# A streaming-encoder trunk: state products in four quadrants of TensorE, a shorter lift of the scan, Toeplitz rows copied in three parts

## The reference

```python
lam_bar = jnp.exp(lam * step)                       # 64 groups x 64 complex states
b_bar = ((lam_bar - 1.0) / lam)[..., None] * b
bu = jnp.einsum('blgn,gpn->blgp', uf, b_bar)        # 16 inputs of a group into its 64 states
_, states = lax.associative_scan(combine, (a, bu), axis=1)      # s[t] = lam_bar * s[t-1] + bu[t]
y = jnp.einsum('gnp,blgp->blgn', c, states).real + d * uf
y = jax.nn.gelu(y.reshape(bsz, seq, D_MODEL))
y = y * jax.nn.sigmoid(y @ glu_w + glu_b)           # the first large product, "GLU"
```

## Time and profile before

| | before |
|---|---|
| median of 3 runs | 1282.84 us |
| the profiled execution, whole | 1282.2 us |
| its span, first to last instruction | 1280.4 us |
| TensorE busy in the span | 97% |
| VectorE, ScalarE, GpSimd busy | 52%, 36%, 5% |
| mean granted TensorE clock | 0.997 of full |
| start of the first GLU product in the span | 105.53 us |

### The profile page before, as it was taken

One profiled execution on the slowest core, in us unless ns is written; L12 is line 12 of the kernel. 1 busy time (PEld: TensorE's weight loads), 2 busy tenths in 40 slices (PEclk: granted clock), 3 DMA queues, 4 the chain that ended last, 5 costly groups with the idle time before them and its releaser, 6 DMA issues.

```text
span 1280.4 us, 16011 instructions
## 1 busy us (share of the span) xinstructions
PE 1247.4 (97%) x6277; PEld 1041.6 (81%) x6277; DVE 671.6 (52%) x785; ACT 462.1 (36%) x486; POOL 64.5 (5%) x79
## 2 busy tenths in 40 slices
PE   3899999999999999999999999999999999999998
PEld 3788888888888888888888888888888888888886
DVE  8996854444444444646556465644454444444443
ACT  5635533333333333333333333422333333332232
POOL 6940000000000000000000000000000000000000
PEclk9999999999999999999999999999999999999999
DMA  5374233232323334322222232223232333323331
GB/s 115 100 133 133 67 117 106 77 104 87 100 76 91 93 109 138 107 66 96 77 81 91 66 106 81 84 84 92 87 106 91 99 98 98 98 68 90 92 110 67
DMA packets 148207, 121.03 MB, mean 95 GB/s; under 512 B 5720, under 2 KB 141072, under 8 KB 148176
## 3 DMA queue, kind: packets, MB, share of 16 engines
q1 hardware_dynamic: 142416, 116.40, 29.6%
q10 hardware_dynamic: 5760, 4.20, 1.7%
HBM read 114.29 MB, written 2.10 MB: 91 GB/s over the span
## 4 chain that ended last, share of the span: by engine, by line
PE 94%; DVE 4%; ACT 1%; issue 0%; DMA 0%; SPq 0%; DVEq 0%
PE bank L701 27%; PE bank L703 27%; PE bank L702 27%; PE bank L800 2%; PE bank L801 2%; PE bank L799 2%; PE bank L647 1%; DVE bank L1169 1%; PE bank L829 1%; PE bank L827 1%; PE bank L828 1%; PE bank L838 1%; ACT s_states L892 1%; PE bank L812 0%; PE bank L813 0%; PE bank L528 0%
## 5 line engine op out<-in xcount | busy, mean ns | idle before, releaser
L701 PE MATMUL bank<-u_hi,w_hi 128*128 128x512 f32 x960 | 375.0, 391 | 0.0
L703 PE MATMUL bank<-u_hi,w_lo 128*128 128x512 f32 x960 | 373.5, 389 | 0.0
L702 PE MATMUL bank<-u_lo,w_hi 128*128 128x512 f32 x960 | 373.5, 389 | 0.0
L1179 DVE TENSOR_TENSOR w_lo<-w_raw,w_hi 128x2048 fp32r<-128x2048 f32 x112 | 256.5, 2290 | 170.3 <-ACT w_hi L892 170.2
L892 ACT ACTIVATE w_hi<-w_raw 128x2048 fp32r<-128x2048 f32 x112 | 213.9, 1910 | 322.3 <-PE bank L703 314.0
L701 PEld LDWEIGHTS bank<-u_hi,w_hi 128*128 128x128 f32 x960 | 180.3, 188 | 37.7 <-issue 0.9
L703 PEld LDWEIGHTS bank<-u_hi,w_lo 128*128 128x128 f32 x960 | 180.2, 188 | 37.7
L702 PEld LDWEIGHTS bank<-u_lo,w_hi 128*128 128x128 f32 x960 | 180.3, 188 | 37.5 <-issue 0.5
L701 PE MATMUL bank<-h_hi,w_hi 128*128 128x512 f32 x352 | 136.9, 389 | 0.0
L702 PE MATMUL bank<-h_lo,w_hi 128*128 128x512 f32 x352 | 136.9, 389 | 0.0
L703 PE MATMUL bank<-h_hi,w_lo 128*128 128x512 f32 x352 | 136.9, 389 | 0.0
(11 more groups left out here) (223 smaller groups left out, 1335.9 us busy)
## 6 DMA issues: line engine op xcount, KB each, us to landing
w_raw<-in_ret_w_qkvg_dram SPq DMA_DIRECT2D x24, 1024.0 KB, 5.0
w_raw<-in_ffn_w_gate_dram SPq DMA_DIRECT2D x22, 1024.0 KB, 5.2
w_raw<-in_ffn_w_up_dram SPq DMA_DIRECT2D x22, 1024.0 KB, 5.2
w_raw<-in_ffn_w_down_dram SPq DMA_DIRECT2D x32, 704.0 KB, 4.3
w_raw<-in_ret_w_o_dram SPq DMA_DIRECT2D x8, 1024.0 KB, 5.1
w_raw<-in_s_glu_w_dram SPq DMA_DIRECT2D x4, 1024.0 KB, 5.6
s<-in_x_dram ACTq DMA_DIRECT2D x8, 256.0 KB, 8.1
s_w<-in_x_dram SPq DMA_DIRECT2D x1, 2048.0 KB, 7.7
```

The lines of the kernel that those rows point to most:

```text
L701: pe.matmul(o, w_hi[w][:, w_cols], hi, start=first, stop=False)
L702: pe.matmul(o, w_hi[w][:, w_cols], lo, start=False, stop=False)
L703: return pe.matmul(o, w_lo[w][:, w_cols], hi, start=False, stop=end)
L1179: dve.tensor_tensor(w_lo[s][:, :], w_raw[:, s, :], w_hi[s][:, :].bitcast(F32), ALU.subtract).then_inc(w_lo_ready[s], 1)
```

## The change

- **State products.** `y_states(quarter, k)` now takes blocks k and k + 2 together. Of blocks 2, 3, 6 and 7 (`swapped`) the output halves are exchanged, so that four matmuls in a row go to four different 64 x 64 quadrants of the array, the two blocks writing two banks. `y_bank` undoes the exchange when the transposed block is read. `SLOT` orders the pairs in `states` so that a quarter of the lift holds blocks 0 and 2, 1 and 3, 4 and 6, 5 and 7.
- **Carries.** They are kept in a small array of their own, `carries`, and GpSimd copies them back to the ends of the segments (2 copies, `ends_ready`, for which `y_states` waits too).
- **Lift.** Three products in place of four: (re + im of the carry) times the real factor, and the carry times the sum and the difference of the factors (`lift_pair`, made before the scan). As instructions: one of 392 elements, three of 784.
- **Segment powers** come one block earlier on GpSimd, ahead of block 2's table, and are copied in the slots' order by 4 small copies. VectorE waits for them before the scan, and makes both `step8` and `step64` there.
- **Toeplitz rows** in three parts, of blocks 0 to 3, 4 and 5, 6 and 7. Both halves of part 0 are SP's, 16 DMAs of 128 KB; of parts 1 and 2 ScalarE issues half 1, 8 DMAs of 64 KB each. The strip of part 0 lies on partitions 0 to 31 over both slots of `w_raw`, those of parts 1 and 2 in slot 1.
- **Weights.** GLU weights go to slot 0 as soon as part 0 has landed, ahead of part 2's DMAs; to slot 1 after parts 1 and 2. VectorE's share of the split of slot 0 comes after `y_low(3)`, ScalarE's after `y_high(3)`.
- **Order.** TensorE: `strips(6)` first, then `y_inputs` 0 to 3, `strips(7)`, `y_inputs` 4, 5, then the two first quarters, `y_transposed` 0 to 3, `y_inputs` 6, 7, the two last quarters, `y_transposed` 4 to 7. The GELUs go 0, 2, 1, 3, 4, 6, 5, 7.

```diff
+SLOT = [0, 2, 1, 3, 4, 6, 5, 7]
-PART = 2 * JB
-NPART = J // PART
+PART_BLOCKS = [(0, 1, 2, 3), (4, 5), (6, 7)]
+PART_OF = [0, 0, 0, 0, 1, 1, 2, 2]
...
-            for part in range(NPART):
-                toeplitz_half(sp, part, 0)
-            for s in range(2):
-                for part in (s, 2 + s):
-                    sp.wait_ge(toep_loaded[part], 16 * 2 * STEPS)
-                load_unit(s, 0, glu_v[:, :, 256 * s:256 * s + 256], KT, 256)
+            toeplitz_half(sp, 0, 0)
+            toeplitz_half(sp, 0, 1)
+            toeplitz_half(sp, 1, 0)
+            sp.wait_ge(toep_loaded[0], 16 * 2 * STEPS)
+            load_unit(0, 0, glu_v[:, :, 0:256], KT, 256)
+            toeplitz_half(sp, 2, 0)
+            for part in (1, 2):
+                sp.wait_ge(toep_loaded[part], 16 * 2 * STEPS)
+            load_unit(1, 0, glu_v[:, :, 256:512], KT, 256)
...
-                        yield 4 * k + i, half, rows64, bank[S5_AT[("y", k)][0]][rows64, P * i:P * i + P]
+                        out0 = 64 * (half ^ swapped(k))
+                        yield 4 * k + i, half, rows64, bank[S5_AT[("y", k)][0]][out0:out0 + 64, P * i:P * i + P]
...
+            def y_states(quarter, k):
+                pe.wait_ge(ends_ready, 2)
+                pe.wait_ge(scan_done, quarter + 1)
+                both = [list(y_pairs(n)) for n in (k, k + 2)]
                 for i in range(4):
                     for ri in range(2):
-                        for jj, half, rows64, o in list(y_pairs(k))[2 * i:2 * i + 2]:
-                            mm = pe.matmul(o, states[rows64, 0:CH, ri, jj], r_tc[rows64, ri, jj, :, :],
+                        for n in range(2):
+                            for jj, half, rows64, o in both[n][2 * i:2 * i + 2]:
+                                at = JB * SLOT[jj // JB] + jj % JB
+                                mm = pe.matmul(o, states[rows64, 0:CH, ri, at], r_tc[rows64, ri, jj, :, :],
...
+            dve.wait_ge(lift_ready, 1)
+            rotation(step8, seg_powers[:, :, 0, :])
+            step(dve.tensor_copy(step64[:, 0], repeated(last_lift[:, 0], 2, 2)))
+            step(dve.tensor_copy(step64[:, 1, :, 0], last_lift[:, 1]))
+            step(dve.tensor_scalar(step64[:, 1, :, 1], last_lift[:, 1], -1.0, None, ALU.mult))
...
+            step(dve.tensor_tensor(lift_pair[:, :, 0, :], lift[1], lift[0], ALU.subtract))
+            step(dve.scalar_tensor_tensor(out=lift_pair[:, :, 1, :], in0=lift[0], scalar=-1.0, in1=lift[1],
...
-            dve.wait_ge(lift_ready, 1)
-            rotation(step64, seg_powers[:, :, SEG - 1, :])
...
+            step(dve.tensor_copy(carries[:, :, 0], ends[:, 0]))
...
+            step(dve.tensor_tensor(carry_sum, carries[:, :, :, 0, :], carries[:, :, :, 1, :], ALU.add))
...
+                step(mul(lift_re, repeated(carry_sum[:, part], 2, M), repeated(seg_powers[:, 0, 0:M, js], 1, M)))
+                step(mul(lift_im, repeated(carries[:, part], 2, M), repeated(lift_pair[:, :, :, js], 1, M)))
+                settle()
+                into = seg[:, 1:SEG, 0:M, :, js]
+                step(dve.tensor_tensor(into, into, repeated(lift_re, 3, 2), ALU.add))
+                settle()
+                dve.tensor_tensor(into, into, lift_im[:, :, :, ::-1, :], ALU.add).then_inc(scan_done, 1)
...
-                if n == 3:
+                if n == 2:
                     segment_powers()
```

More of the change, by code:

```diff
@@ L409, in tile, with swapped, y_bank @@
             return t[:, bass.ds(k, 1), :].rearrange("p o a -> p (o a)")
+        def swapped(k):
+            return k // 2 % 2
         def y_part(t, k):
             jb = k // 2
[L415 removed]
+            whole = t[:, jb:jb + 5:4, :].rearrange("p h (c t) -> p h c t", t=STEPS)
+            return whole[:, :, :, 4 * (k % 2):4 * (k % 2) + 4]
+        def y_bank(k):
+            ps = bank[S5_AT[("yt", k)][0]].rearrange("p (t h c) -> p h c t", t=4, h=2)
+            return ps[:, ::-1, :, :] if swapped(k) else ps
         def toeplitz_half(queue, part, half):
[L419 removed]
+            for k in PART_BLOCKS[part]:
                 b, fill = S5_AT[("strip", k)]
                 queue.wait_ge(bank_free[b], fill + 1)
[L422 to L423 removed]
+            g0 = J * half + JB * PART_BLOCKS[part][0]
+            n = JB * len(PART_BLOCKS[part])
             for r in range(STEPS):
                 at = LEAD - N * r
[L426 to L427 removed]
+                queue.dma_start(toep[N * r:N * r + N, g0:g0 + n, :],
+                                strip[part][N * half:N * half + N, :, at:at + P]).then_inc(toep_loaded[part], 16)
         @block.sync
@@ L666, in y_inputs @@
                     pe.matmul(o, u[:, jj, half, :], toep[:, J * half + jj, :], start=(jj % 4 == 0), stop=False)
+            strips(6)
             pe.wait_ge(toep_loaded[0], 16 * 2 * STEPS)
@@ L670, in _ @@
             y_inputs(1)
-            strips(6)
             pe.wait_ge(seg_done, 1)
-            pe.wait_ge(toep_loaded[1], 16 * 2 * STEPS)
             y_inputs(2)
@@ L1014, in y_high @@
                 ps, _ = s5_full("yt", k)
-                copy(y_part(g_hi, k), ps[:, :].rearrange("p (t h c) -> p h c t", t=4, h=2)).then_inc(y_hi_ready, 1)
+                copy(y_part(g_hi, k), y_bank(k)).then_inc(y_hi_ready, 1)
+            for k in (0, 2, 1, 3):
+                gelu(k)
             for k in range(4):
-                gelu(k)
+                y_high(k)
             split_weights(0, 0)
-            for k in range(4, 8):
-                if k % 2 == 0:
-                    y_high(k - 4)
-                    y_high(k - 3)
+            for k in (4, 6, 5, 7):
                 gelu(k)
@@ L1675, in _ @@
             pool.memset(fb[:, :, :, :], 0.0).then_inc(fb_zeroed, 1)
-            for s in range(2):
-                zeroed = pool.memset(strip[:, s, :, 0:LEAD], 0.0)
+            pool.memset(strip_wide[:, :, 0:LEAD], 0.0)
+            zeroed = pool.memset(strip_slot1[:, :, 0:LEAD], 0.0)
             zeroed.then_inc(pads_zeroed, 1)
@@ L1740, in segment_powers @@
             def segment_powers():
-                step(pool.tensor_copy(seg_powers[:, :, 0, :], powers[:, :, STEPS, :]))
+                for ri in range(2):
+                    for part in range(2):
+                        js = slice(16 * part, 16 * part + 16)
+                        step(pool.tensor_copy(seg_powers[:, ri, 0, js].rearrange("p (c b d) -> p b c d", c=2, b=2),
+                                              powers[:, ri, STEPS, js].rearrange("p (b c d) -> p b c d", b=2, c=2)))
                 settle()
@@ L1772, in _ @@
                 pool.wait_ge(tc_ready, 2 * n + 2)
+            pool.wait_ge(seg_done, 2)
+            ends = states[:, 1:CH + 1, :, :].rearrange("p (s i) r j -> p s i r j", s=SEG)[:, 1:SEG - 1, SEG - 1, :, :]
+            for ri in range(2):
+                pool.tensor_copy(ends[:, :, ri, :].rearrange("p s (q j) -> p s q j", q=4),
+                                 carries[:, :, 1:SEG - 1, ri, :].rearrange("p q s j -> p s q j")).then_inc(ends_ready, 1)
+            pool.wait_ge(ends_ready, 2)
 _INS = ["x", "s5_norm", "s5_lambda_re", "s5_lambda_im", "s5_log_step", "s5_b_re", "s5_b_im", "s5_c_re", "s5_c_im",
```

113 lines of the change are left out of this document (46 added, 67 removed).

## The result

The changed kernel takes **1294.42 us** (median of 4 runs, 1293.58 to 1294.68), the kernel before 1282.65 in the runs beside it: a ratio of 1.0091, 95% interval 1.0080 to 1.0103. It is 11.8 us slower where 5.5 us of gain were forecast.

What follows compares the result with a forecast made beforehand. TensorE's queued work behind VectorE's scan bounds the first GLU product; quadrants, lift and copies move it from 105.5 to 100.0 us, 5.5 us off 1282.2, plus 0.6 for the median: 1277.3 us, range 1274.9 to 1283.3.

Steps and rivals of the forecast that it cites:

- the part on the Toeplitz rows: Part 0's copies on SP: 2.1 MB at 145 to 190 GB/s take 11 to 14.5 us from 60.3, landed at 74.5.
- upper bound: Latest landing of part 0's copies: issues of 1.23 us each, then a landing of 3.5, giving 83.5 us.
- rival 3: Part 0 lands late: each us after 75.1 delays the GLU one us, up to 1285.7 us; chance 0.08.
- Rival 2: TensorE's clock falls behind new waits, 2.8 us ahead of strips(6) and smaller ones later: 1278.5 to 1281 us; chance 0.15.
- four quadrants: TensorE's state products: 64 records in 2.1 us instead of 3.84, saving 7 us of TensorE's work after 82.86.
- rival 1: State products: four quadrants run no faster than two, 3.84 us per double block; 1283.0 us, no change; chance 0.15.
- the lift: VectorE's lift of a quarter takes 3.5 us instead of 4.26; the last ends at 92.8, 2.7 us earlier.
- ScalarE's second eight copies: ScalarE's eight DMAs after strips(7) take 5.2 to 6.2 us, to 87.7, followed at once by the GELUs.
- the rigid shift of all that follows the GLU's start: From the first GLU product TensorE runs without a gap, so what its start gains, the end gains.
- the start of the scan: VectorE's scan starts at 54.13 as before; 1.4 us of added work hides in a 1.79 us wait for ScalarE.
- VectorE's second `lift_pair` operation: One of two operations of 224 elements ahead of VectorE's scan, taken at 0.4 us each and hidden.
- the copy of the carries: VectorE's added copy behind the scan, taken at 0.25 us, ahead of the first quarter's lift.

Runs made afterwards that it cites:

- a3: The changed kernel with part 1's halves swapped, SyncE issuing half 1 and ScalarE half 0: 1290.5 us (one run).
- c3: The changed kernel with part 0's half 1 issued by ScalarE beside SyncE's half 0, both in the same order of r: 1286.0 us (one run).
- a1: The changed kernel with the 16 copies of part 0 alternating between the halves, still all on SyncE: 1286.39 us.
- d1: The changed kernel with the earlier four-part Toeplitz copies, ScalarE's half 1 in order r = 4..7, 0..3, and all of part 0 on SyncE: 1278.66 us.
- d2: d1 with VectorE's two lift_pair operations moved behind carry_sum and GpSimd's strip memsets behind its first lam products: 1280.89 us.
- f1: d1 with part 0's half 1 copied before half 0, and y_inputs(0) and (1) ahead of strips(6): 1277.81 us.

## Why the prediction was wrong

- **The step that failed** is in the part on the Toeplitz rows: "I take the bytes as the bound and the middle of them: landed at 74.5". The bytes were taken at 145 to 190 GB/s, "what these copies reached with both queues at work". In the earlier trace rows that was the rate of two halves read at once, and the change makes them follow each other: 98 GB/s, `y_inputs(0)` at 90.07. (The middle of 11 and 14.5 us behind 60.3 would be 73; the prediction doesn't say what the 1.4 us up to 74.5 are.) That alone is 15.0 of the 18.1 us by which the GLU started later than forecast.
- **Its upper bound failed too.** 83.5 took the slowest issue of the earlier trace rows, 1.23 us. But the issue is not a cost of its own: here it took 1.33 and 2.05 us, the time of the copies ahead of it. A bound from the rate of one queue was at hand in the earlier trace rows, 97 GB/s from 66 to 68 with SyncE alone: 2.1 MB by that are 21.6 us, landed at about 82. It was read there for its clock. The rest is ScalarE's 0.5 MB of part 1 out of the same limit: 2.6 MB at 98 GB/s from 61.48 on would be through at 88.3 (an estimate), and in a3, without this sharing, `y_inputs(0)` started at 86.19.
- **The argument against rival 3** was "one queue and two share the same 16 engines". But the engines were not the limit: the DMA share was 0.78 at 98 GB/s, and 1.25 at 140 in c3. Rival 3 had the right place, and its rule, each us of lateness one us for the GLU, held but for the 3.1 us that came on top (15.0 and 18.1). Its chance, 0.08, was far too low.
- **Rival 2, the lower clock, came on top of it.** The wait ahead of `strips(6)` that it named is there, 2.73 us, and `strips(6)` took 3.52 us for 1.93, hidden here. Behind the late part 0 the inputs took 5.57 for 3.7, and behind the wait of 2.74 us for the GELUs the transposes took 2.57 for 2.0 and inputs 6 and 7 2.98 for 1.97. The sum behind `y_inputs(0)` was 24.9 us and is 28.0.
- **Right**: four quadrants, 1.97 us for 64 records (2.1 taken), so rival 1 is out; the lift, 3.50 us from quarter to quarter (3.5), in the rows below; ScalarE's second eight copies, 6.12 us, and the GELUs right behind them; the rigid shift of all that follows the GLU's start.
- **Too small, and hidden here**: the start of the scan, forecast unchanged at 54.13, came at 55.84. VectorE's second `lift_pair` operation took 1.46 us where 0.4 was taken, and the copy of the carries 0.75 for 0.25. Of the 1.7 us, 1.2 are not the pair's: ScalarE had the last states that the scan needs out at 55.23, and at 54.02 before; in a1 they are out at 54.27, and the scan starts at 54.71. VectorE's timeline, with the starts of two lift quarters, and GpSimd's beside it:

```profile
53.97 0.45 DVE L1380 TENSOR_TENSOR s<-s_seg_powers 128x224 f32<-128x224 f32 x1
54.34 1.46 DVE L1381 SCALAR_TENSOR_TENSOR s<-s_seg_powers 128x224 f32<-128x224 f32 x1
55.84 1.23 DVE L1188 TENSOR_TENSOR bank<-s_states,bank 128x1024 f32<-128x1024 f32 x1
...
74.77 0.75 DVE L1409 COPY s<-s_states 128x64 f32<-128x64 f32 x1
...
88.20 0.57 DVE L1188 TENSOR_TENSOR s<-s,s_seg_powers 128x392 f32<-128x392 f32 x1
...
91.70 0.57 DVE L1188 TENSOR_TENSOR s<-s,s_seg_powers 128x392 f32<-128x392 f32 x1
```

```profile
54.13 1.42 POOL L1793 TENSOR_TENSOR s_tc<-s_pool_tmp,s_seg_tmp 128x512 f32<-128x512 f32 x1
```

GpSimd's operation at 54.13 (1.42 us) runs just there. The Trainium skill, "SBUF — State Buffer", section "Who interferes with whom", says that a VectorE instruction with two SBUF inputs contends with a GpSimd instruction that reads SBUF, and that the lock is exclusive. The trace agrees: the two operations of equal size take 0.45 and 1.46 us here, 1.39 and 1.28 in d1, and 0.53 each in d2, where they stand behind the carries and GpSimd's tables are done. (Beside the second pair in d2 run two short copies of GpSimd's, 0.95 us together, and no such delay shows.)
- **The weights and the first 50 us**: the weights are not late. But the two memsets of the strips ran from 2.48 to 4.88, 0.77 longer than before, which was not costed. The issue of x for the transposes is at 51.44, 1.2 us later than before; in a1, whose first 50 us are the same code, it is at 50.49, so most of this is a difference between executions.
- **The sum without the fault**: with scan, lift and quadrants as changed and the groups kept apart, f1 reaches 1277.8 us, where 1277.3 was forecast. It does so in four parts and another order, with waits and a lower clock that the sum doesn't have, so this shows that the gain is there to be had. That the two numbers are so near is luck, and proves no term.
